# Sums of squares in two fp32r passes, attention products issued in pairs, and projection inputs moved 192 bytes

## The reference

```python
s = einsum("bthd,bshd->bhts", qi, k) * scale + (cqi[..., :, None] - c_k[..., None, :])
p = softmax(where(kpos <= qpos, s, -inf))
out = einsum("bhts,bshd->bthd", p, v)
```

```python
def rms_norm(t, g):
    tf = t.astype(float32)
    y = tf * rsqrt(mean(tf * tf, axis=-1, keepdims=True) + 1e-6)
    return y * g
```

## Time and profile before

| | us |
|---|---|
| median of 3 runs | 2857.57 |
| lowest and highest | 2854.04, 2860.43 |
| the profiled execution | 2857.84 |
| span of its trace | 2856.1 |
| TensorE busy in the span | 2740.0 |
| VectorE | 1703.8 |
| ScalarE | 1043.3 |
| GpSimd | 931.4 |

### The profile page before, as it was taken

One profiled execution on the slowest core, in us unless ns is written; L12 is line 12 of the kernel. 1 busy time (PEld: TensorE's weight loads), 2 busy tenths in 40 slices (PEclk: granted clock), 3 DMA queues, 4 the chain that ended last, 5 costly groups with the idle time before them and its releaser, 6 DMA issues. The chain is left out here.

```text
span 2856.1 us, 39411 instructions
## 1 busy us (share of the span) xinstructions
PE 2740.0 (96%) x15534; PEld 2109.4 (74%) x15534; DVE 1703.8 (60%) x2674; ACT 1043.3 (37%) x1727; POOL 931.4 (33%) x549
## 2 busy tenths in 40 slices
PE   6999999999999899999999999988999999999999
PEld 5979797987878677777776887755666667776777
DVE  5787878786121344444546113676776686677686
ACT  4342434343110133333324002335666654444231
POOL 2232323232565111111112333533322233333465
PEclk9999999999999999999999999999999999999999
DMA  4131423232633111111112323521101101112643
GB/s 169 52 94 67 84 72 83 73 77 102 216 111 115 45 46 49 39 44 53 53 42 104 111 74 125 194 102 44 40 27 44 38 19 56 42 42 92 217 147 108
DMA packets 113751, 236.53 MB, mean 83 GB/s; under 512 B 9120, under 2 KB 52896, under 8 KB 113568
## 3 DMA queue, kind: packets, MB, share of 16 engines
q1 hardware_dynamic: 63312, 172.14, 18.3%
q10 hardware_dynamic: 50256, 61.87, 7.2%
HBM read 189.88 MB, written 44.11 MB: 82 GB/s over the span
## 5 line engine op out<-in xcount | busy, mean ns | idle before, releaser
L80 PE MATMUL psum<-u_h,w_hi 128*128 128x512 f32 (+2 forms) x2624 | 1014.0, 386 | 21.4 <-DVE u_h L2929 6.2
L82 PE MATMUL psum<-u_h,w_lo 128*128 128x512 f32 (+2 forms) x2624 | 965.0, 368 | 0.0
L81 PE MATMUL psum<-u_h,w_hi 128*128 128x512 f32 (+2 forms) x2624 | 962.5, 367 | 0.0
L136 POOL TENSOR_SCALAR w_hi<-w_raw 128x1024 fp32r<-128x1024 f32 x212 | 234.7, 1107 | 1424.9 <-ACTq L1346 515.7
L80 PEld LDWEIGHTS psum<-u_h,w_hi 128*128 128x128 f32 x2624 | 497.7, 190 | 153.5 <-issue 74.9
L81 PEld LDWEIGHTS psum<-u_h,w_hi 128*128 128x128 f32 x2624 | 498.4, 190 | 71.5 <-issue 11.5
L138 POOL TENSOR_TENSOR w_lo<-w_raw,w_hi 128x1024 fp32r<-128x1024 f32 x212 | 545.1, 2571 | 17.7
L82 PEld LDWEIGHTS psum<-u_h,w_lo 128*128 128x128 f32 x2624 | 497.2, 189 | 71.6
L1371 ACT ACTIVATE f_exp<-psum 128x1024 f32<-128x1024 f32 (+5 forms) x104 | 78.8, 775 | 247.5 <-PE psum L1221 110.2
L2589 ACT ACTIVATE a_exp<-a_exp 128x1024 f32<-128x1024 f32 x96 | 101.4, 1056 | 118.9 <-DVE a_exp L2761 61.2
L1465 DVE CUSTOM_DVE_ANT_0 f_junk<-psum,f_decay,f_max 128x512 f32<-128x512 f32 (+2 forms) x96 | 60.3, 665 | 128.7 <-PE psum L1249 102.3
(11 more groups left out here) (431 smaller groups left out, 4424.0 us busy)
## 6 DMA issues: line engine op xcount, KB each, us to landing
w_raw<-in_w_all SPq DMA_DIRECT2D x212, 512.0 KB, 3.5
sums_rows<-s_acs ACTq DMA_DIRECT2D x32, 512.0 KB, 8.6
f_decay<-s_nc SPq DMA_DIRECT2D x16, 520.0 KB, 5.8
s_y<-conv_out ACTq DMA_DIRECT2D x16, 512.0 KB, 2.9
yo_raw<-s_y ACTq DMA_DIRECT2D x8, 1024.0 KB, 9.6
x_tok<-in_x SPq DMA_DIRECT2D x8, 512.0 KB, 8.1
s_xT<-xT SPq DMA_DIRECT2D x8, 512.0 KB, 4.9
s_pssd<-fox_last ACTq DMA_DIRECT2D x16, 256.0 KB, 2.2
```

What stands on the lines that cost most here:

```text
L80: nc.tensor.matmul(out, w_hi[:, k], a_hi, start=(k == 0 and first), stop=False)
L81: nc.tensor.matmul(out, w_hi[:, k], a_lo, start=False, stop=False)
L82: return nc.tensor.matmul(out, w_lo[:, k], a_hi, start=False, stop=(k == kk - 1 and final))
L136: self.nc.gpsimd.tensor_scalar(self.hi[:, r], self.raw[:, r], 1.0, 1.0, ALU.mult, ALU.mult).then_inc(self.hi_done, 1)
```

## The change

1. **fox_phase.** `MULTIPLIED` says which units' values a step issues: step 1 those of units 0 and 1, step 3 of 2 and 3, and so on to step 10, which has unit 10 alone. `pt` has three buffers, and the waits of `exps` go back by one more unit.
2. **u_hi, u_lo.** The used 1040 columns of each block of 1088 begin at column 48, not 0. With the 16 columns of META the halves begin at column 64 of a block.
3. **mixers_phase, sums of squares.** For q of 1 to 7, four groups each (28 in all), ScalarE squares the bank twice, into `a_sq` and, rounded to fp32r, into the hi slot of the keys or queries to come; VectorE subtracts the second from the first into the lo slot (`low_square`); and TensorE sums the two parts with two fp32r matmuls with `pairs_r`. The four sums of q = 0 stay as they were. `low_square` stands at the end of VectorE's step in which the group's projection ends.
4. **finish** of the pass before moves from step 3 to step 2 in dilated passes on VectorE.

The diff, without its new declarations:

```diff
+    MULTIPLIED = {1: [0, 1], 3: [2, 3], 5: [4, 5], 7: [6, 7], 9: [8, 9], 10: [10]}
-        pt = sb("f_exp", [P, 2, 2, 512])
+        pt = sb("f_exp", [P, 3, 2, 512])
...
-                    values(p, x, more)
+                    for y in MULTIPLIED.get(x, []):
+                        values(p, y, more)
...
-                act.wait_ge(pv_ok, p * NU + x - 1 + NU)
-                act.wait_ge(acc_ok, gathered(p, x - 1))
+                act.wait_ge(pv_ok, p * NU + x - 2 + NU)
+                act.wait_ge(acc_ok, gathered(p, x - 2))
...
+        squares = lambda c: c + 1 if c < 4 else 2 * c - 3
+        pairs_r = sb("pairs_r", [P, P], F32R)
...
+        shaped_as = lambda q, t: t if diff(q) else classes(t)
+        square_rows = lambda q, g, i: ((k_hi, k_lo) if g <= GK1 else (q_hi, q_lo))[i][:, q % 2]
...
                 if kind == "S":
-                    pe.wait_ge(sq_ok, number_of(q, g) + 1)
-                    last = nc.tensor.matmul(bank, K.pairs[:, :], sq[:, number_of(q, g) % 2], start=True, stop=True)
+                    if q == 0:
+                        pe.wait_ge(sq_ok, number_of(q, g) + 1)
+                        last = nc.tensor.matmul(bank, K.pairs[:, :], sq[:, number_of(q, g) % 2], start=True, stop=True)
+                    else:
+                        pe.wait_ge(const_ok, 2)
+                        pe.wait_ge(sqlo_ok, number_of(q, g) - 3)
+                        for i in range(2):
+                            last = nc.tensor.matmul(shaped_as(q, bank), pairs_r[:, :], square_part(q, g, i), start=(i == 0), stop=(i == 1))
...
                     nc.scalar.activation(sq[:, c % 2], gbank(n), ACT.Square).then_inc(sq_ok, 1)
+                    if q:
+                        least(act, st_ok, base(q - 1))
+                        nc.scalar.activation(square_part(q, g, 0), shaped_as(q, gbank(n)), ACT.Square).then_inc(sq_ok, 1)
...
+            def low_square(q, g):
+
+                c = number_of(q, g)
+                dve.wait_ge(sq_ok, squares(c) + 1)
+                tt(square_part(q, g, 1), shaped_as(q, sq[:, c % 2]), square_part(q, g, 0).bitcast(F32), ALU.subtract).then_inc(sqlo_ok, 1)
...
-                    if p >= 1 and x == 3:
+                    if p >= 1 and x == (3 if diff(p) else 2):
                         finish(p - 1, 1)
...
+                    for g, k in share(q, x) if 0 < q < PASSES else []:
+                        if k == KT - 1 and g <= GQ1:
+                            low_square(q, g)
+                    for g, k in early(p, x):
+                        if k == KT - 1:
+                            low_square(1, g)
...
-        u_hi, u_lo = (uh[:, i * KT * LP:(i + 1) * KT * LP].rearrange("p (k t) -> p k t", k=KT) for i in range(2))
+        u_hi, u_lo = (uh[:, i * KT * LP:(i + 1) * KT * LP].rearrange("p (k t) -> p k t", k=KT)[:, :, LP - L:LP] for i in range(2))
```

More of the change, by code:

```diff
@@ L1271, in values @@
                         last = nc.tensor.matmul(ps[64 * j:64 * j + 64, OB + q0 - 512 * h:OB + 512], V[0:n, kb, j],
-                                                pt[0:n, (p * NU + x) % 2, j, at:end], start=(kb == 0), stop=(kb == 4 + 3 * h))
+                                                pt[0:n, (p * NU + x) % 3, j, at:end], start=(kb == 0), stop=(kb == 4 + 3 * h))
                 last.then_inc(pv_ok, 1)
@@ L1370, in exps @@
                 for n, a, e in [(P, full[-1][4], 512)] + [(META, b[4], b[5]) for b in bs if b[2] == META]:
-                    last = nc.scalar.activation(pt[0:n, (p * NU + x) % 2, :, a:e], src[0:n, :, a:e], ACT.Exp, scale=0.125)
+                    last = nc.scalar.activation(pt[0:n, (p * NU + x) % 3, :, a:e], src[0:n, :, a:e], ACT.Exp, scale=0.125)
                 last.then_inc(exp_ok, 1)
@@ L1472, in accumulate @@
                 for m, (h, kb, n, q0, at, end) in enumerate(blocks(x)):
-                    to, src = acc[0:n, h, :, q0 - 512 * h:512], pt[0:n, (p * NU + x) % 2, :, at:end]
+                    to, src = acc[0:n, h, :, q0 - 512 * h:512], pt[0:n, (p * NU + x) % 3, :, at:end]
                     if kb == 0:
@@ L2051, in mixers_phase @@
         tok_ok = s("tokens")
+        sqlo_ok = s("square_lo")
+        squares = lambda c: c + 1 if c < 4 else 2 * c - 3
+        pairs_r = sb("pairs_r", [P, P], F32R)
         rootx, invx, scalex, addx_ok, sqx_ok, sumx = (s(n) for n in ["rootx", "invx", "scalex", "addx", "sqx", "sumx"])
@@ L2094, in mixers_phase @@
         y2 = lambda it: sq[:, 1] if it[0] == "N" else vT[:, 0] if it[2] == GQ1 else den[:, :]
+        shaped_as = lambda q, t: t if diff(q) else classes(t)
+        square_rows = lambda q, g, i: ((k_hi, k_lo) if g <= GK1 else (q_hi, q_lo))[i][:, q % 2]
+        square_part = lambda q, g, i: (square_rows(q, g, i)[:, 512 * (g % 2):512 * (g % 2) + 512] if diff(q)
+                                       else classes(square_rows(q, g, i))[:, :, P * (g % 2):P * (g % 2) + P])
         sqx = lambda k: (acc0[:, 1], zT[:, 3], V[:, 4:8].rearrange("p c t d -> p (c t d)"))[k % 3]
@@ L2350, in scores @@
                 if X == 0:
-                    pe.wait_ge(const_ok, 1)
+                    pe.wait_ge(const_ok, 2)
                     pe.wait_ge(ttr_ok, 10)
@@ L2912, in _ @@
             nc.vector.memset(halves[:, :], -0.5 * EPS)
+            nc.vector.tensor_copy(pairs_r[:, :], K.pairs[:, :]).then_inc(const_ok, 1)
             nc.vector.memset(ek[:, :].bitcast(F32), 0.0)
@@ L2918, in _ @@
             last.then_inc(const_ok, 1)
-            dve.wait_ge(const_ok, 1)
+            dve.wait_ge(const_ok, 2)
             dve.wait_ge(par_in, 32)
```

## The result

| | before | changed |
|---|---|---|
| median of the runs side by side | 2859.03 us | 2880.99 us |
| lowest and highest | 2854.04, 2863.12 | 2871.49, 2881.72 |
| ratio, with its 95% interval | | 1.0078 (1.0067 to 1.0089) |
| span of the trace | 2856.1 us | 2878.1 us |

A forecast was written before the change was run, and what follows sets the result against it. TensorE was taken as the bound, busy 2740 of 2856.1 us. Pairs -6, columns -4, sums -11.2, waits +19.0 and clock +5 gave +2.8, to 2860.6 us, predicted as 2861, range 2849 to 2870.

The forecast's parts named there:

- values in pairs: Attention in fox_phase: 40 groups of values standing behind another group save 0.17 us each, taken as -6 us, bounds -4 and -7.
- columns: State-space phase and fox_phase: 2304 matmuls on realigned halves save 0.0023 us each, taken as -4 us; thirds 0, bounds -9 and +4.
- sums, saved: Mixers: two fp32r matmuls in place of the float32 sum save 0.40 us on each of 28 sums, -11.2 us.
- wait at GQ0, four passes: Differential passes: TensorE waits 3.4 us each for low_square, which ends behind GpSimd's subtraction of the weights, +13.6 us.
- wait at GQ1, four passes: Differential passes: the subtraction barely fits before the sum, 0.1 to 0.6 us each, taken as 0.3, +1.2 us.
- GQ0, three dilated passes: Dilated passes: low_square ends with GpSimd's rounding or 0.5 us later, 0.85 to 1.4 us of wait each, +3.6 us.
- finish: Dilated passes: moved one step earlier to make room for the subtraction, hidden in VectorE's idle time, 0 us.
- clock in the mixers: The clock halves behind three of the four 3.4 us waits, up to 1.7 us lost each, +5 us, bounds 0 and 6.8.
- rival 1: Mixers: the subtraction precedes GpSimd or the port is free; four waits of 1.3 us, clock stays up, 2847 us; chance 0.18.
- Rival 3: Mixers' sums: two fp32r matmuls save only 0.2 us because the first is slow, 2866 us; chance 0.06.
- Rival 2: Same wait, clock falls in all four passes (+1.8), halves' offset not the cause (+4): 2866.4, or 2870 with worse thirds; chance 0.16.
- the forecast, 2856 to 2867: Whole kernel: the main case's span of times, varying by the clock and GQ1; chance 0.52.

The follow-up runs named there:

- the two at other offsets: Kernel before with the used columns of u_hi and u_lo begun at column 16 or 32, one run each; halves in the merge step by 232.9 and 233.3 ns.
- the last of the experiments on the keys: Kernel before with values in pairs and two fp32r passes for the keys' sums alone, q = 1's GK0 left in float32; 2847.04 us, 0.9968.

## Why the prediction was wrong, point by point

| term | forecast | measured in the traces |
|---|---|---|
| values in pairs | -6 | -7.2 |
| columns | -4 | +2.1 |
| sums, saved | -11.2 | 0.40 each, as forecast |
| wait at GQ0, four passes | +13.6 | 3.3, 3.4, 3.4, 4.2 = +14.3 |
| wait at GQ1, four passes | +1.2 | 1.1, 1.1, 1.1, 0.3 = +3.6 |
| GQ0, three dilated passes | +3.6 | 3 x 1.1 = +3.3 |
| GQ1, three dilated passes | none | 3 x 0.4 = +1.3 |
| first keys | +0.6 | one wait of 2.3 in place of two (0.6 and 1.3), +0.3 |
| finish | 0 | +2.0 |
| clock in the mixers | +5 | 14.0 - 1.5 = +12.5 |

The mixers by this table: 22.5 + 0.3 + 2.0 + 12.5 - 11.2 = 26.1, measured 25.7. Over all rows the misses add up to 18 of the 19 us between the forecast's +2.8 and the traces' +22.

**Right:** the pairs; the price of the sum, 1.20 to 0.80; and the main step, that `low_square` doesn't get in ahead of GpSimd's subtraction of the weights and ends with it. The earlier trace rows were the right witness, the wait came out at 3.4, and rival 1 was rightly held to be unlikely. Rival 3 didn't happen.

**Wrong: the clock**, the largest miss, 7.5 us. I took three half clocks of four. All four came, one of them twice as long; and I priced it only for these waits, although three more waits became long enough or moved: behind the first exponentials (wait 2.3), at 2356.6, behind a wait of 2.1 that stood there before without it, and at the last chain. Rival 2 put 1.8 on top, since it also counted four places only. One of the extra pieces is chance, as far as the runs show: the second trace of the changed kernel has 3.4 us less at half.

**Wrong: finish.** I wrote "hidden in VectorE's idle time, 0". In the last pass, which projects for no further one, nothing needs the room, and finish stands there ahead of what the next projection waits for. I had looked at a dilated pass in the middle and taken it for all. That is 2.0 us of wait; the longer half clock behind it is not tied to it by any run.

**Wrong: the columns.** The halves went the way of the earlier trace rows. The term that failed is the thirds, of which "no row tells": 0 with 0.0015 either way, and it was 0.0022 up on 2200 recorded steps, outside the bound. The bound had no row behind it. And the halves gained 1.4 ns on the mean of the state-space phase, not 2.3.

**Wrong: GQ1.** 0.71 us of room for 0.68 was read with GpSimd left out. The earlier trace rows had shown for GQ0 how a neighbour on GpSimd stretches it; the same question was not asked at GQ1, where its low rows run 0.1 us ahead. In the dilated passes I named no wait for GQ1 at all; `low_square` there starts only behind ScalarE's copy and VectorE's norms, and ends 0.4 late.

**Wrong: the range.** 2849 to 2870 was taken from the rivals one at a time. The terms' own bounds at their dear end (pairs +2, columns +8, a saving of 0.2 a sum +5.6, clock +1.8, GQ1 +1.2) already make 2879. Nor do the clock and GQ1 reach 2867, as "the forecast, 2856 to 2867" says: with their upper bounds the sum is 2863.6.

What lay ahead of the mixers came out at -3.6, where pairs and steps make -5.1; the 1.5 us between them were not traced further.

## What to carry to other kernels

A saving of 0.4 us a sum is safe only where its new inputs have room: of four sums a pass the two of the keys had it and the two of the queries had not. With the keys' sums alone, the columns back and the pairs kept, 22 us more became 9 less, of which the pairs alone give 8. For each subtraction that is added on VectorE, look at every place where it will stand, at what GpSimd runs in that microsecond, and at what comes next in VectorE's queue, since a hold on GpSimd moves the collision to the next operation. Where TensorE gets a new wait of a length that had a half clock behind it in the traces (here 25 of 33 from 2.0 to 2.9 us), count the clock's price as likely for each such wait, not as certain, and look for waits elsewhere that grow.

## What the runs showed of the hardware

- **Half clock at a wait.** In the mixers of fourteen traces (before, changed, and the experiments but the two at other offsets), from the first pass's exponentials on: of 30 waits of TensorE of 3.3 us or longer, the same five places in six traces, all had a granted clock of 0.50 (1.2 GHz, not 2.4) around or behind them; of 33 from 2.0 to 2.9 us 25; of 21 from 1.6 to 1.8 us 2. The same wait of 2.1 us had it in some kernels and not in others. Length alone doesn't decide for longer ones either: at the first mark four of the kernels wait 3.2 to 3.3 us and run on at 1.00, here the last of the experiments on the keys:

```profile
1938.01 0.50 PE L2360 MATMUL psum<-a_khi,a_qhi 64*128 64x512 f32 x2 [3.24 <-POOL a_klo L2236]
```

```profile
1938.01:1941.42 3.41, 3.41 (x19) 2.05 (x19) 2.40 (x5) 0.00 (x0) 3.33 (x2) 1.00 0.00 0
```

- **A VectorE operation of 0.15 us took 1.59** when GpSimd's subtraction of 128 x 1024 was running, in each of four passes of two kernels: the price is GpSimd's rest, not a factor on VectorE's own time.
- **The start of a matmul's moving columns** changes its step by up to 6.6 ns of 227 at 512 columns, and thirds and halves differ in which start suits them.
